# Router logits from the raw stream, an fp32 gather in two halves and a tenth expert slot in a two-block kernel

## The chip, the cores and the metric

The kernel runs on one core of one Trainium2 chip. The metric is the device time of one execution in microseconds, lower is better. A core has a tensor engine (PE), a vector engine (DVE), a scalar engine (ACT), GpSimd (POOL) and a sync engine (SP), which here issues nearly all transfers from memory. Each engine runs its own list of instructions in order; semaphores tie the lists together. Sixteen DMA engines carry the transfers.

## What is computed

256 tokens of width 1024 go through two blocks. The first puts 16 meta tokens ahead, normalizes, mixes (a gated delta rule and a stick-breaking attention), normalizes again and sends every token to 2 of 32 experts; the second is an attention, a squared-relu MLP, a pooling mixer and another MLP. The change lies between the first block's mixer and the end of its experts:

```python
h = layer_norm(DEEPNORM_ALPHA * h + mix, ln1_g[i], ln1_b[i])
ffn = hierarchical_moe(h, ...)
h = layer_norm(DEEPNORM_ALPHA * h + ffn, ln2_g[i], ln2_b[i])
# hierarchical_moe: 4 groups of 8 experts, t = h as tokens
group_probs = softmax(t @ router_group_w + router_group_b); g_idx = argmax(group_probs)
exp_logits = einsum("td,gde->tge", t, router_expert_w) + router_expert_b
top_logit, top_idx = top_k(exp_logits of group g_idx, 2)
top_w = softmax(top_logit) * max(group_probs)
for each expert e: hid = silu(t @ w_gate[e]) * (t @ w_up[e]); y += (hid * weight of e) @ w_down[e]
```

An expert has three fp32 matrices of 1 MB; all 32 are read.

## The kernel before

**Expert stage.** Every expert has 32 places (`CAP`) for its tokens; four experts make a quad, eight quads (`QUADS`) make the stage, two quads a pair. The order is quad 0, quad 1, a spill expert (one expert may have up to 128 more tokens), then quads 2 to 7 (`ORDER`). Of a quad PE computes the up products (L1088, 128x32 tiles, four experts side by side), a turn of the hidden values (L1107, L1111), the down products (L1125) and, after the next quad's up products, the scatter of the result into banks 0 to 3 (L1148), where it is added to the residual stream that `carry` (L1029) has put there through products with the identity. The tokens of a pair come into the expert order by a gather (`gather`, L1057): a product of the normalized stream with a 0/1 matrix `sel` made by `select` (L2170). The stream is held as a rounded part `hiX` (L1606, ACT, in X1) and a remainder `loX` (L2122, DVE, in xT), and the gather multiplies both, each in single-pass fp32r, 256 columns wide. DVE (L2188) and ACT (L1626) copy the four banks to `xs` with scale and shift of the layer norm. `gather_spill` (L1067) does the same for the spill expert right behind quad 0's up products.

**Weights.** They come in units of 2 MB, each two loads of 1024 KB (the second spill unit is half as large): a quad has four up units and two down units, so 48 and 2 of spill. `moe_load` (L530) issues them on SP in the order of use. Seven slots (`MOE_SLOTS`) go round, four in `ring` and three in the arena, and two more places (`once`, in params and in X1 with X2) are used once, so nine units are fetched ahead, in the order `FIRST_USE`, as the mixer's last matrices free their places. After that unit j waits until semaphore `moe_unit` says that the unit seven earlier is used up. `moe_unit` rises by one with each expert's last up product and by two with a quad's down products.

**From the mixer to the experts.** PE ends the `mixed` products (L1010). DVE adds them to the stream and takes statistics (L2100 to L2103), normalizes (L1834); PE fills with four products (`keep_going`, L621), transposes the normalized stream (L628), ACT (L1612) and DVE (L2115) copy it to `xs` with ln1's gain and shift, PE multiplies by the router matrix `wr` (L1023), DVE picks groups, two experts and the membership (L2128 to L2155), makes the remainder of the second tile (L2122), PE counts ranks (L1037 to L1041), DVE makes `select(0)`, PE gathers pair 0. `turned_act`, `turned_dve`, `res` and `four_psum` are counters that later stages use too.

## Time and profile before

| | us |
|---|---|
| median of 3 runs | 1057.35 |
| lowest and highest | 1052.74, 1062.34 |
| the profiled execution | 1054.88 |
| its span in the profile | 1052.8 |
| PE busy in the span | 963.3 (91%) |
| DVE busy | 527.8 (50%) |
| ACT busy | 381.0 (36%) |
| mean granted TensorE clock | 0.965 of full |

The profile is of one execution. The span is the time from its first to its last instruction. Chain of waits means the chain of work that ended last, followed back from the last instruction; a load's piece there is the time from its issue to its landing. PE's fp32 products leave two records each, fp32r products and transposes one. The rows that matter are in the section before the prediction.

### The profile page before, as it was taken

Reading aid. Unit: us, or ns where it says so; the run is one execution under the profiler, and the core shown is the slowest. Engines: PE = TensorE matmul, PEld = TensorE weight load, DVE = VectorE, ACT = ScalarE, POOL = GpSimd, SP = SyncE. Lnnn points to the kernel's source line nnn. Section 1 sums busy time; section 2 is a strip of 40 time slices with the busy share of each in tenths; the row PEclk is TensorE's granted clock in tenths of the full one; section 3 lists DMA queues with packets and bytes.
Section 4 is the critical chain, followed back from the end, with each engine's and each line's share of the span. In section 5 each row is a group of like instructions: output and inputs, shape, how many; then the busy total and the mean of one; then the engine's idle time right before and its main releaser. Section 6 shows DMA issues by size and latency. Waiting matters only on the chain.

```text
span 1052.8 us, 14462 instructions
## 1 busy us (share of the span) xinstructions
PE 963.3 (91%) x6163; PEld 738.7 (70%) x6163; DVE 527.8 (50%) x799; ACT 381.0 (36%) x478; POOL 35.7 (3%) x51
## 2 busy tenths in 40 slices
PE   8999989999999985656979999999999989999997
PEld 7998776455775422213327888899899879999995
DVE  5883463186655102001029568465554665546554
ACT  4554302954322100001036556333433444334341
POOL 1400100012000000000000000000000000000000
PEclk9999999999989988878999999999999999999999
DMA  9733420433773999999997650454554544545421
GB/s 334 235 120 121 160 83 1 151 140 128 301 303 143 416 422 420 422 421 421 421 397 277 209 190 1 182 219 161 192 207 160 173 160 147 199 162 224 172 80 40
DMA packets 67273, 229.42 MB, mean 218 GB/s; under 512 B 4096, under 2 KB 5408, under 8 KB 54544
## 3 DMA queue, kind: packets, MB, share of 16 engines
q1 hardware_dynamic: 65360, 223.28, 55.7%
q0 software_dynamic: 1632, 5.26, 1.5%
q8 instruction: 42, 0.69, 0.3%
q14 instruction: 15, 0.12, 0.0%
q10 hardware_dynamic: 224, 0.07, 0.0%
HBM read 227.54 MB, written 1.05 MB: 217 GB/s over the span
## 4 chain that ended last, share of the span: by engine, by line
PE 80%; DMA 11%; DVE 5%; issue 1%; ACT 1%; SPq 1%; ACTq 0%; DVEq 0%
PE bank L1345 17%; PE bank L1356 16%; PE bank L1088 6%; DMA ring<-in_expert_w_up 5%; PE bank L682 5%; PE bank L706 5%; PE bank L1225 4%; DMA arena<-in_expert_w_up 3%; PE bank L695 3%; PE bank L1010 2%; PE bank L971 2%; PE bank L1287 2%; DMA arena<-in_expert_w_down 2%; PE bank L1229 2%; PE bank L1125 2%; PE bank L715 1%
## 5 line engine op out<-in xcount | busy, mean ns | idle before, releaser
L2341 DVE TENSOR_TENSOR w_lo<-ring,w_hi 128x2048 fp32r<-128x2048 f32 x76 | 170.6, 2288 | 88.1 <-ACT w_hi L1670 87.9
L1670 ACT ACTIVATE w_hi<-ring 128x2048 fp32r<-128x2048 f32 x76 | 141.1, 1909 | 92.8 <-PE bank L1356 86.9
L1345 PE MATMUL bank<-xT_hi,w_hi 128*128 128x256 f32 x512 | 143.8, 281 | 2.6 <-DVE xT_lo L2329 2.6
L1345 PE MATMUL bank<-xT_hi,w_lo 128*128 128x256 f32 x512 | 143.6, 280 | 0.0
L1345 PE MATMUL bank<-xT_lo,w_hi 128*128 128x256 f32 x512 | 143.2, 280 | 0.0
L1356 PE MATMUL bank<-w_hi,hidden_lo 128*128 128x512 f32 x256 | 99.9, 390 | 0.0
L1356 PE MATMUL bank<-w_lo,hidden_hi 128*128 128x512 f32 x256 | 99.8, 390 | 0.0
L1356 PE MATMUL bank<-w_hi,hidden_hi 128*128 128x512 f32 x256 | 99.6, 389 | 0.0
L1345 PEld LDWEIGHTS bank<-xT_hi,w_hi 128*128 128x128 f32 x512 | 96.2, 188 | 3.5 <-issue 3.0
L1345 PEld LDWEIGHTS bank<-xT_lo,w_hi 128*128 128x128 f32 x512 | 96.4, 188 | 0.5
L1345 PEld LDWEIGHTS bank<-xT_hi,w_lo 128*128 128x128 f32 x512 | 95.9, 187 | 0.0
L1088 PE MATMUL bank<-ring,arena 128*32 128x512 f32 x256 | 67.6, 683 | 22.4 <-DMA arena<-in_expert_w_up 22.4
L1088 PE MATMUL bank<-arena 128*32 128x512 f32 x224 | 60.5, 708 | 24.3 <-DMA ring<-in_expert_w_up 24.3
L2239 DVE TENSOR_TENSOR X<-X,bank 128x256 f32<-128x256 f32 x9 | 3.8, 420 | 114.5 <-ACT X L1637 114.5
L1766 ACT ACTIVATE arena<-bank 128x512 f32<-128x512 f32 x32 | 19.2, 600 | 113.1 <-PE bank L1345 113.1
L2442 DVE TENSOR_TENSOR arena<-arena 128x512 f32<-128x512 f32 x32 | 22.1, 690 | 66.8 <-ACT arena L1766 66.8
L1356 PEld LDWEIGHTS bank<-w_hi,hidden_lo 128*128 128x128 f32 x256 | 48.0, 188 | 10.1
L1356 PEld LDWEIGHTS bank<-w_lo,hidden_hi 128*128 128x128 f32 x256 | 48.1, 188 | 9.7
L1356 PEld LDWEIGHTS bank<-w_hi,hidden_hi 128*128 128x128 f32 x256 | 48.1, 188 | 9.6
L1088 PEld LDWEIGHTS bank<-arena 128*32 128x32 f32 x224 | 15.2, 128 | 48.4 <-issue 48.4
L706 PE MATMUL bank<-ring,xT 128*128 128x512 f32 x112 | 48.3, 593 | 0.8 <-issue 0.8
L1637 ACT ACTIVATE X<-bank 128x256 f32<-128x256 f32 x9 | 3.5, 385 | 125.1 <-PE bank L1088 118.7
(527 smaller groups left out, 1675.3 us busy)
## 6 DMA issues: line engine op xcount, KB each, us to landing
ring<-in_mlp_w_up SPq DMA_DIRECT2D x32, 1024.0 KB, 6.9
ring<-in_mlp_w_down SPq DMA_DIRECT2D x32, 1024.0 KB, 6.3
ring<-in_w_in SPq DMA_DIRECT2D x22, 1024.0 KB, 7.5
ring<-in_expert_w_down SPq DMA_DIRECT2D x22, 1024.0 KB, 19.4
ring<-in_expert_w_gate SPq DMA_DIRECT2D x16, 1024.0 KB, 13.8
ring<-in_expert_w_up SPq DMA_DIRECT2D x16, 1024.0 KB, 15.9
arena<-in_expert_w_gate SPq DMA_DIRECT2D x15, 1024.0 KB, 12.3
arena<-in_expert_w_up SPq DMA_DIRECT2D x15, 1024.0 KB, 14.3
```

Of the source, the lines that this page charges most:

```text
L682: last = mm(B[n % 4][:, 0:L], w_[:, k * 512 + c * P:k * 512 + (c + 1) * P], x_[:, k, :], start=(p_ == 0 and k == 0), stop=(p_ == 2 and k = ...
L695: last = mm(B[n % 4][0:r, :], x_[:, k, a:a + r], w_[:, k * 512:(k + 1) * 512], start=(p_ == 0 and k == 0), stop=(p_ == 2 and k == KD - 1))
L706: last = mm(B[n % 4][0:r, :], xT[:, k, a:a + r], slab(u, k), start=(k == 0), stop=(k == KD - 1))
L971: last = mm(B[n], x_(2 * part + kk, i), w_[:, kk * D + half * 512:kk * D + (half + 1) * 512], start=(part == 0 and p_ == 0 and kk == 0), s ...
L1010: last = mm(B[2 * (u - 13) + i], x_, w_, start=(part == 0 and p_ == 0 and kk == 0), stop=(part == 1 and p_ == 2 and kk == 3))
L1088: last = mm(cube(B[4][CAP * e:CAP * (e + 1), :], 2), xs[:, k, (q % 2) * P + CAP * e:(q % 2) * P + CAP * (e + 1)], w_[e][:, :, k, :], start ...
L1225: mm(bank, x_[:, k, i * P:(i + 1) * P], w_hi[:, k * 512:(k + 1) * 512], start=(k == 0 and x_ is xTH), stop=False)
L1345: last = mm(B[4 + (2 * j + pr) % 4][:, cc * SEQ:(cc + 1) * SEQ], w_[:, k * 512 + c * P:k * 512 + (c + 1) * P], x_[:, k, 0:SEQ], start=(k = ...
L1356: last = mm(B[n], h_[:, j % 2, c, i * P:(i + 1) * P], w_[:, c * D + half * 512:c * D + (half + 1) * 512], start=(first and c == 0 and p_ = ...
L1670: act(whi[:, n % 2, half], slot(u)[:, half], ACT.Copy).then_inc(S("split_hi"), 1)
L2341: tt(wlo[:, u % SLOTS, half], slot(u)[:, half], f32(whi[:, n % 2, half]), ALU.subtract).then_inc(S("split_lo"), 1)
L2442: tt(r_, r_, r_, ALU.mult).then_inc(S("square_steps"), 1)
```

## The change

1. **Logits from the raw stream.** PE transposes the stream before it is normalized, as soon as DVE has added the mixer's output (`res` now counts this too, so later uses of `res` are shifted by two), ACT copies it to `xs` unscaled, and PE multiplies by `wr`, which DVE has multiplied by ln1's gain in an earlier stage. DVE then corrects the product: logit = product times 1/std, plus `logit_0`, which is made of mean, 1/std and the column sums `row_1` and `row_0` of the two scaled router matrices. The sums over partitions are one more PE product beside the decay products of the mixer, with a wait for `g_made` 3.
2. **The normalized transposes** for `carry` follow behind the router products, and ACT alone scales all four banks of them. `carry(0)` is split around the rank products; `carry(1)` moves behind quad 0's up products.
3. **fp32 gather.** `hiX` and `loX` are gone. ACT makes a permuted fp32 copy `xhatP` in X1, and the gather multiplies it with an fp32 `sel` in ordinary fp32. The first pair's gather goes in two halves of 128 columns, the second behind quad 0's up products. `gather_spill` moves behind quad 1's up products.
4. **A tenth slot.** xT's place is now free: X0 and the first 2048 columns of xT make a fourth `spare`, `MOE_SLOTS` is 8, and ten units are fetched ahead. The tenth waits for both permuting copies and for the transposes. Thresholds of SP's waits follow from the eight slots. In the overflow case, which these inputs don't take, the sum is kept in X2 instead of X0.
5. **Filling products.** `keep_going(4)` ahead of the transposes and single ones before and after the ranks are gone; ahead of the last quad stand 22 of 128 columns instead of 6 of 512.

In the diff below unchanged lines are left out, and so are hunks that only follow (counter offsets, slot views with the two halves of a unit as a dimension, `pair_weighed`).

```diff
--- before.py
+++ after.py
@@ -230,13 +230,13 @@
...
-    hiX = parts("h1_hi", "X1", 0, NT * D).rearrange("p (i k c) -> p i k c", i=NT, k=KD)
-    loX = parts("h1_lo", "xT", 0, NT * D).rearrange("p (i k c) -> p i k c", i=NT, k=KD)
+    xhatP = X1[:, 0:NT, :].rearrange("p i (k c) -> p i k c", k=KD)
+    spare_sum = cube(X2[:, :], NT)
+    row_1, row_0, row_sums = arena[:, 18820:18856], arena[:, 18856:18892], arena[:, 18892:18964]
+    wr_b, logit_0 = cube(arena[:, 18964:18964 + KD * 36], KD), cube(arena[:, 19252:19324], NT)
...
-    sel = cube(parts("select", "arena", 0, NT * PAIR), NT)
-    reg(NT * PAIR)
-    sel_spill = cube(parts("select_spill", "arena", taken["arena"], NT * SPILL), NT)
-    reg(NT * SPILL)
+    sel = cube(reg(NT * PAIR), NT)
+    sel_spill = cube(reg(NT * SPILL), NT)
...
@@ -331,13 +332,15 @@
...
-    MOE_SLOTS = 7
+    MOE_SLOTS = 8
...
-    once = (params[:, :, :].rearrange("p a d -> p (a d)"), nc.alloc_sbuf_tensor_at("X1_X2", [P, UNIT], F32, offset=placed["X1"] + 4 * NT * D)[:, :])
-    spare = [arena[:, SPARE + a * UNIT:SPARE + (a + 1) * UNIT] for a in range(3)]
-    FIRST_USE = [8, 5, 6, 7, 2, 3, 0, 1, 4]
+    once = (params[:, :, :].rearrange("p (b a) d -> p b (a d)", b=2), nc.alloc_sbuf_tensor_at("X1_X2", [P, 2, HALF_U], F32, offset=placed["X1"] + 4 * NT * D)[:, :, :])
+    spare = [cube(arena[:, SPARE + a * UNIT:SPARE + (a + 1) * UNIT], 2) for a in range(3)]
+    X0_TO_XT = (placed["xT"] - placed["X0"]) // 4
+    spare.append(nc.alloc_sbuf_tensor_at("X0_xT", [P, 2, X0_TO_XT], F32, offset=placed["X0"])[:, :, 0:HALF_U])
+    FIRST_USE = [2, 6, 7, 8, 3, 4, 0, 1, 5, 9]
...
@@ -348,7 +351,7 @@
...
-        return once[m - MOE_SLOTS] if m >= MOE_SLOTS else spare[m - 3] if 3 <= m < 6 else ring[:, {6: 3}.get(m, m), :]
+        return once[m - MOE_SLOTS] if m >= MOE_SLOTS else spare[m - SLOTS] if m >= SLOTS else cube(ring[:, (m + 3) % SLOTS, :], 2)
...
@@ -521,13 +531,16 @@
...
-            elif j in (5, 6, 7):
+            elif j in (6, 7, 8):
...
+            elif j == 9:
+                sp.wait_ge(S("permuted"), NT)
+                sp.wait_ge(S("four_psum"), 8)
...
-                of = U_TWO - 4 + (8, 2, 3, 4).index(j)
+                of = U_TWO - 4 + (2, 3, 4, 5).index(j)
...
-                sp.dma_start(moe_slot(s_, j)[:, a:a + src.shape[1]], src).then_inc(S(f"moe_in{moe_at(s_, j)}"), 16)
+                sp.dma_start(moe_slot(s_, j)[:, a // HALF_U, a % HALF_U:a % HALF_U + src.shape[1]], src).then_inc(S(f"moe_in{moe_at(s_, j)}"), 16)
...
@@ -547,7 +560,7 @@
...
-                sp.wait_ge(S("moe_unit"), FIRST - 6 + (u - U_TWO))
+                sp.wait_ge(S("moe_unit"), FIRST - 7 + (u - U_TWO))
...
@@ -746,8 +759,10 @@
...
-        mm(B[5][:, 24:25], C("mones"), G[:, 8:9], start=True, stop=True).then_inc(S("dec_psum"), 1)
-        pe.wait_ge(S("rows_made"), 1)
+        mm(B[5][:, 24:25], C("mones"), G[:, 8:9], start=True, stop=True)
+        pe.wait_ge(S("g_made"), 3)
+        mm(B[5][:, 32:104], C("ones"), row_sums, start=True, stop=True).then_inc(S("dec_psum"), 1)
+        pe.wait_ge(S("g_made"), 2)
...
@@ -1013,25 +1028,29 @@
...
-        keep_going(4)
-        turn(X0, "xhat", 0, "four_psum")
-        pe.wait_ge(S("router_in"), 16 * (NG + 5))
-        for k in range(KD):
-            if k % 2 == 0:
-                turned(1, k // 2)
-            for i in range(NT):
+        for i in range(NT):
+            pe.wait_ge(S("res"), i + 1)
+            for k in range(KD):
+                last = tr(B[4 + 2 * i + k // 4][:, (k % 4) * P:(k % 4 + 1) * P], X0[:, i, k * P:(k + 1) * P], ident)
+                if k % 4 == 3:
+                    last.then_inc(S("xT_psum"), 1)
+        for i in range(NT):
+            for k in range(KD):
+                if k % 4 == 0:
+                    pe.wait_ge(S("xT_act"), 5 + 2 * i + k // 4 + 1)
...
-        def carry(i):
-            for k in range(KD):
-                mm(B[2 * i + k // 4][:, (k % 4) * P:(k % 4 + 1) * P], xs[:, k, i * P:(i + 1) * P], ident, start=(k % 4 == 0), stop=False)
-        carry(1)
+        turn(X0, "xhat", 0, "four_psum")
+        def carry(i, blocks):
+            for b in blocks:
+                pe.wait_ge(S("turned_act"), 4 + b + 1)
+                for k in (2 * b, 2 * b + 1):
+                    mm(B[2 * i + k // 4][:, (k % 4) * P:(k % 4 + 1) * P], xs[:, k, i * P:(i + 1) * P], ident, start=(k % 4 == 0), stop=False)
...
-        carry(0)
-        keep_going(1)
+        carry(0, (0, 1))
...
@@ -1039,32 +1058,33 @@
...
+        carry(0, (2, 3))
...
-            pe.wait_ge(S(name), total(s_, 9, 8, n // 2 + 1))
-        def gather(s_, p):
-            pe.wait_ge(S("sel_made"), pair_made(s_, p))
+            pe.wait_ge(S(name), total(s_, GATHERS // 2, 2 * NG, n // 2 + 1))
+        def gather(s_, p, first=0, width=PAIR, shift=0):
+            pe.wait_ge(S("sel_made"), pair_made(s_, p) - (1 if width < PAIR and first == 0 else 0))
...
-                    gathered(s_, gather_index(s_, p, 0))
+                    gathered(s_, shift + gather_index(s_, p, 0))
...
+                    at = kk * PAIR + first
...
-                        for m, x_ in enumerate((hiX, loX)):
-                            last = mm(B[(5, 6, 7, 5)[b]][:, kk * PAIR:(kk + 1) * PAIR], x_[:, i, 2 * b + kk, :], sel[:, i, :], start=(i == 0 and m == 0), stop=(i == NT - 1 and m == 1))
+                        last = mm(B[(5, 6, 7, 5)[b]][:, at:at + width], xhatP[:, i, 2 * b + kk, :], sel[:, i, first:first + width], start=(i == 0), stop=(i == NT - 1))
...
-            pe.wait_ge(S("sel_made"), 2)
+            pe.wait_ge(S("sel_made"), 3)
...
+                gathered(None, SECOND + 1 + n)
...
-                        for m, x_ in enumerate((hiX, loX)):
-                            last = mm(B[6 + n][:, c * P:(c + 1) * P], x_[:, i, 4 * n + c, :], sel_spill[:, i, :], start=(i == 0 and m == 0), stop=(i == NT - 1 and m == 1))
+                        last = mm(B[6 + n][:, c * P:(c + 1) * P], xhatP[:, i, 4 * n + c, :], sel_spill[:, i, :], start=(i == 0), stop=(i == NT - 1))
...
@@ -1168,15 +1195,20 @@
...
+                    carry(1, range(4))
+                    gather(None, 0, P, P, SECOND)
+                if q == 1 and s_ is None:
...
+                    gathered(None, SPILL_AT)
+                    gathered(None, SPILL_AT + 1)
...
-                    gathered(None, 4)
-                    gathered(None, 5)
+                    gathered(None, SECOND + 1)
+                    gathered(None, SECOND + 2)
...
@@ -1598,38 +1629,38 @@
...
-        deviation(6, slice(1, 3))
-        def rounded(i):
+        for i in range(NT):
+            for b in range(2):
+                sc.wait_ge(S("xT_psum"), KD + 2 * i + b + 1)
+                act(xs[:, 4 * b:4 * b + 4, i * P:(i + 1) * P], cube(B[4 + 2 * i + b], 4), ACT.Copy).then_inc(S("xT_act"), 1)
+            if i == 0:
+                deviation(6, slice(1, 3))
+        for i in range(NT):
...
-            act(hiX[:, i], X0[:, i, :].rearrange("q (p k) -> q k p", k=KD), ACT.Copy).then_inc(S("h1_round"), 1)
-        rounded(0)
-        for b in (0, 2):
+            act(xhatP[:, i], X0[:, i, :].rearrange("q (p k) -> q k p", k=KD), ACT.Copy).then_inc(S("permuted"), 1)
+        for b in range(4):
...
-        rounded(1)
...
-        def gathered(s_, n, dst, bk, k0):
-            sc.wait_ge(S("xs_psum"), total(s_, 18, 16, n + 1))
+        def gathered(s_, n, dst, bk, k0, apart, first=0):
+            sc.wait_ge(S("xs_psum"), total(s_, GATHERS, 4 * NG, n + 1))
...
-                k, w = k0 + j, dst.shape[2]
-                last = act(dst[:, j, :], bk[:, j * w:(j + 1) * w], ACT.Identity, scale=slot_g[:, k:k + 1], bias=slot_b[:, k:k + 1])
+                k, at, w = k0 + j, j * apart + first, dst.shape[2]
+                last = act(dst[:, j, :], bk[:, at:at + w], ACT.Identity, scale=slot_g[:, k:k + 1], bias=slot_b[:, k:k + 1])
...
-        def gather(s_, p):
+        def gather(s_, p, first=0, width=PAIR, shift=0):
...
-                gathered(s_, gather_index(s_, p, b), xs[:, 2 * b:2 * b + 2, :], B[(5, 6, 7, 5)[b]], 2 * b)
+                gathered(s_, shift + gather_index(s_, p, b), xs[:, 2 * b:2 * b + 2, first:first + width], B[(5, 6, 7, 5)[b]], 2 * b, PAIR, first)
...
@@ -1907,7 +1943,13 @@
...
-        last.then_inc(S("rows_made"), 1)
+        last.then_inc(S("g_made"), 1)
+        per_row = lambda name: by_feature[name].unsqueeze(2).broadcast_to([P, KD, 36])
+        dve.wait_ge(S("router_in"), 16 * (NG + 5))
+        line(tt(wr_b, wr, per_row("ln1_b"), ALU.mult))
+        line(nc.vector.reduce_sum(row_sums[:, 36:72], wr_b.rearrange("p k n -> p n k"), AX.X))
+        line(tt(wr, wr, per_row("ln1_g"), ALU.mult))
+        nc.vector.reduce_sum(row_sums[:, 0:36], wr.rearrange("p k n -> p n k"), AX.X).then_inc(S("g_made"), 1)
...
@@ -1917,6 +1959,8 @@
...
+        nc.vector.tensor_copy(row_1, B[5][:, 32:68])
+        line(tt(row_0, B[5][:, 68:104], rbias, ALU.add))
...
@@ -2097,7 +2141,11 @@
...
-            line(stt(x, x, ALPHA, B[n], ALU.mult, ALU.add))
+            if half:
+                stt(x, x, ALPHA, B[n], ALU.mult, ALU.add).then_inc(S("res"), 1)
+                dve.wait_ge(S("res"), i + 1)
+            else:
+                line(stt(x, x, ALPHA, B[n], ALU.mult, ALU.add))
...
@@ -2108,24 +2156,15 @@
...
+            dve.wait_ge(S("xT_psum"), KD + 2 * i + 2)
...
-        for b in (1, 3):
-            dve.wait_ge(S("four_psum"), 4 + b + 1)
-            for k in (2 * b, 2 * b + 1):
-                last = ts(xs[:, k, :], B[4 + b][:, (k % 2) * SEQ:(k % 2 + 1) * SEQ], by_feature["ln1_g"][:, k:k + 1], by_feature["ln1_b"][:, k:k + 1], ALU.mult, ALU.add)
-            last.then_inc(S("turned_dve"), 1)
-        def low_part(i):
-            dve.wait_ge(S("xhat"), i + 1)
-            dve.wait_ge(S("h1_round"), i + 1)
-            tt(loX[:, i], X0[:, i, :].rearrange("q (p k) -> q k p", k=KD), f32(hiX[:, i]), ALU.subtract).then_inc(S("h1_low"), 1)
-        low_part(0)
-        dve.wait_ge(S("router_in"), 16 * (NG + 5))
+        line(stt(mean_rst, mv[:, 1:1 + NT, 0], -1.0, rst[:, 1:1 + NT], ALU.mult, ALU.mult))
+        for i in range(NT):
+            last = stt(logit_0[:, i, :], row_1, mean_rst[:, i:i + 1], row_0, ALU.mult, ALU.add)
+        line(last)
...
-            last = tt(lg[:, i, :], B[i][:, 0:36], rbias, ALU.add)
+            last = stt(lg[:, i, :], B[i][:, 0:36], rst[:, 1 + i:2 + i], logit_0[:, i, :], ALU.mult, ALU.add)
...
@@ -2154,20 +2193,18 @@
...
-        low_part(1)
...
-        line(nc.vector.tensor_copy(counts, B[4][:, 64:96]))
-        def select(p):
+        def select(p, first=0, n=8):
...
-                slots = C("iota")[:, 0:CAP].unsqueeze(1).broadcast_to([P, 8, CAP])
-                last = tt(cube(sel[:, i, :], 8), slots, rank[:, i, 8 * p:8 * p + 8].unsqueeze(2).broadcast_to([P, 8, CAP]), ALU.is_equal)
+                slots = C("iota")[:, 0:CAP].unsqueeze(1).broadcast_to([P, n, CAP])
+                at = slice(8 * p + first, 8 * p + first + n)
+                last = tt(cube(sel[:, i, CAP * first:CAP * (first + n)], n), slots, rank[:, i, at].unsqueeze(2).broadcast_to([P, n, CAP]), ALU.is_equal)
...
@@ -2175,25 +2212,28 @@
...
-                last = tt(cube(selw[:, i, :], 8), cube(f32(sel[:, i, :]), 8), w_, ALU.mult)
+                last = tt(cube(selw[:, i, :], 8), cube(sel[:, i, :], 8), w_, ALU.mult)
...
-        select(0)
-        def gathered(s_, n, dst, bk, k0):
-            dve.wait_ge(S("xs_psum"), total(s_, 18, 16, n + 1))
+        select(0, 0, 4)
+        select(0, 4, 4)
+        nc.vector.tensor_copy(counts, B[4][:, 64:96]).then_inc(S("router_dve"), 1)
+        dve.wait_ge(S("router_dve"), 5)
+        def gathered(s_, n, dst, bk, k0, apart, first=0):
+            dve.wait_ge(S("xs_psum"), total(s_, GATHERS, 4 * NG, n + 1))
...
-                k, w = k0 + j, dst.shape[2]
-                last = ts(dst[:, j, :], bk[:, j * w:(j + 1) * w], slot_g[:, k:k + 1], slot_b[:, k:k + 1], ALU.mult, ALU.add)
+                k, at, w = k0 + j, j * apart + first, dst.shape[2]
+                last = ts(dst[:, j, :], bk[:, at:at + w], slot_g[:, k:k + 1], slot_b[:, k:k + 1], ALU.mult, ALU.add)
...
-        def gather(s_, p):
+        def gather(s_, p, first=0, width=PAIR, shift=0):
...
-                gathered(s_, gather_index(s_, p, b), xs[:, 2 * b:2 * b + 2, :], B[(5, 6, 7, 5)[b]], 2 * b)
-        gather(None, 0)
+                gathered(s_, shift + gather_index(s_, p, b), xs[:, 2 * b:2 * b + 2, first:first + width], B[(5, 6, 7, 5)[b]], 2 * b, PAIR, first)
+        gather(None, 0, 0, P)
...
@@ -2238,7 +2278,9 @@
...
-                gathered(None, 5, xs_spill[:, 4:8, :], B[7], 4)
+                gather(None, 0, P, P, SECOND)
+            if q == 1 and s_ is None:
+                gathered(None, SPILL_AT + 1, xs_spill[:, 4:8, :], B[7], 4, P)
...
```

## Rows read from the trace of the kernel before

**Rows 1.** The page: busy tenths of the DMA engines, 40 slices of 26.3 us
```profile
DMA  9733420433773999999997650454554544545421
```
**Rows 2.** Windows: stretch, length, busy us by engine, clock, DMA share, GB/s
```profile
316.60:334.00 17.40, 16.93 (x138) 10.46 (x136) 12.43 (x49) 3.91 (x7) 0.00 (x0) 1.00 0.07 15
334.00:538.50 204.50, 148.46 (x925) 60.98 (x924) 23.33 (x62) 22.48 (x45) 0.00 (x0) 0.87 1.01 419
...
332.60:338.00 5.40, 4.36 (x40) 4.09 (x44) 2.49 (x9) 2.49 (x6) 0.00 (x0) 1.00 0.82 284
```
**Rows 3.** Timeline of SP: start, us, issuing line, what it loads, loads merged (x)
```profile
302.81 0.99 SPq L530 DMA_DIRECT2D ring<-in_expert_w_down  x2
332.66 0.33 SPq L530 DMA_DIRECT2D ring<-in_expert_w_gate  x1
...
333.50 8.78 SPq L530 DMA_DIRECT2D ring<-in_expert_w_down  x4
```
**Rows 4.** Chain of waits, 300 to 400 us: start, us, engine and line
```profile
307.58 4.89 PE bank L1023 x32
...
321.52 4.04 PE bank L1057 x32
325.56 7.00 PE bank L1088 x64
332.56 3.73 PE bank L1067 x32
...
337.79 3.64 PE bank L1125 x32
...
348.29 3.96 PE bank L1057 x32
352.26 3.43 PE bank L1148 x8
...
379.12 10.09 PE bank L1088 x64
```
**Rows 5.** The same chain, 400 to 550 us
```profile
517.57 20.95 DMA arena<-in_expert_w_down
...
538.65 5.33 PE bank L1125 x32
```
**Rows 6.** Timeline of DVE and ACT, 298 to 321 us, with idle time before and releaser
```profile
300.48 0.69 DVE L2100 SCALAR_TENSOR_TENSOR X<-X,bank 128x512 f32<-128x512 f32 x1 [1.05 <-PE bank L1010]
...
304.41 2.12 ACT L1606 ACTIVATE h_hi<-X 128x1024 fp32r<-128x1024 f32 x1 [1.94 <-DVE X L1834]
...
306.43 1.92 ACT L1612 ACTIVATE arena<-bank,small 128x256 f32<-128x256 f32 x4
...
312.57 0.30 DVE L2128 TENSOR_TENSOR arena<-bank,arena 128x36 f32<-128x36 f32 x2 [2.73 <-PE bank L1023]
...
317.36 2.00 DVE L2122 TENSOR_TENSOR h_lo<-X,h_hi 128x1024 fp32r<-128x1024 f32 x1
...
320.71 0.76 DVE L2170 TENSOR_TENSOR select<-cst,arena 128x256 fp32r<-128x256 f32 x2
```
**Rows 7.** Chain of waits, 0 to 140 us: fp32 products of 272 and of 128 columns
```profile
17.67 14.67 PE bank L715 x64
...
126.77 1.79 PE bank L785 x16
```
**Rows 8.** Table by windows, around the fall of the granted clock
```profile
306.60:309.90 3.30, 2.32 (x21) 2.35 (x22) 3.24 (x4) 3.30 (x5) 0.00 (x0) 1.00 1.02 429
...
309.90:316.60 6.70, 6.70 (x33) 6.70 (x33) 3.33 (x20) 1.90 (x3) 0.00 (x0) 0.50 1.01 426
```
**Rows 9.** DVE's timeline and the chain of waits near 80 us
```profile
76.87 4.50 DVE L1869 TENSOR_TENSOR w_lo<-ring,first_hi 128x2048 fp32r<-128x2048 f32 x2 [1.01 <-ACT first_hi L1452]
...
86.62 11.12 PE bank L695 x48
```

More of the change, by code:

```diff
@@ L1078, in up_quad @@
         def up_quad(s_, q):
+            if q == 0 and s_ is None:
+                pe.wait_ge(S("router_dve"), 5)
             j = moe_unit(s_, q)
@@ L1119, in down_quad @@
                 moe_landed(s_, j + i)
-            w_ = [moe_slot(s_, j + e // 2)[:, (e % 2) * HALF_U:(e % 2 + 1) * HALF_U] for e in range(4)]
+            w_ = [moe_slot(s_, j + e // 2)[:, e % 2, :] for e in range(4)]
             for half in range(2):
@@ L1649, in experts @@
         def experts(s_, order):
-            gather(s_, 0)
+            if s_ is None:
+                gather(None, 0, 0, P)
+            else:
+                gather(s_, 0)
             for q in order:
```

71 lines of the change are left out of this document (41 added, 30 removed).

## The prediction

> **What bounds the kernel now.** I read the page first. TensorE is 91% busy over the span, but in the middle of the DMA row, from about 330 us to 550 us, every slice but one says 9 [rows 1]. That is the expert stage. The table by windows says it more sharply: from 334.0 to 538.5 us the DMA share is 1.01 at 419 GB/s, while PE is busy for 148 of 204.5 us and at a mean granted clock of 0.87; just ahead of it, from 316.6 to 334.0, the DMA share is 0.07 [rows 2]. So the stage is a full transfer queue that starts late. The reader should see both: a resource with no slack at all for 200 us, and 16 us before it in which the same resource does nothing.
>
> The queue on SP tells why it is empty. The last of nine prefetched units (a unit is 2 MB, two loads of 1024 KB) is issued at 302.81; the next issue is at 332.66 [rows 3], when the first quad's up products end (325.56 + 7.00) [rows 4]: all slots are full until then. In the chain of waits the stage ends with a load issued at 517.57 that lands 20.95 us later, and the down products that it releases at 538.65 [rows 5]. After that the chain is PE work that the change doesn't touch. From the issue at 332.66 to the landing at 538.52 are 205.9 us for what was left. That is 8 quads of 6 units and 2 spill units, one of them half, less 9, is 40.5 units, so **5.08 us a unit**, waits and start included. The end of the stage therefore moves by (change of the restart) + 5.08 us for every unit fetched before it.
>
> **The change, part by part.**
>
> *The tenth slot.* Unit 9 goes behind unit 5, into X0 and the head of xT, which the low part used to hold. SP waits for `permuted` (two permuting copies of 2.12 us on ACT, which begin at 304.41 when the first normalized tile is there [rows 6], so until about 308.7) and for the last transposes. The three units issued from 300.5 to 303.8 keep the queue at work to about 316.6, so unit 9 follows without a hole and lands about 321.7, far ahead of the restart: 39.5 units are left instead of 40.5, **−5.1 us**. It costs nothing on SP, since nothing else is queued behind it but loads that wait for the restart.
>
> *The way to the restart.* Before: the last `mixed` product, statistics, xhat, transposes, scaling copies, router products from 307.58 (4.89 us), logits at 312.57 on DVE, membership, a low part of 2.00 us from 317.36, ranks, select at 320.71 for 0.76 us, gather 321.52 for 4.04 us, up products [rows 4, 6]. After, on the same time axis:
> 1. Raw transposes follow the products: the second tile's residual is made 300.48 to 301.17 [rows 6], so 16 transposes at 0.11 us end by 302.2. ACT's four copies (at most two of L1612's pieces, 0.96 us, each) stay ahead of PE or close to it.
> 2. Router products, 32 passes. At the full clock 21 of them fit in the 2.3 us up to 309.9 (0.11 us each), the other 11 took 2.6 us at half clock [rows 4, 8]. From 302.2: 305.7 at full clock, 307.8 if the clock falls at 303.2. The new correction (three DVE operations of about 0.2 us behind xhat, done at 305.8) is hidden there. Logits at 305.95: 6.6 us earlier.
> 3. DVE from logits to membership, 317.36 − 312.57 = 4.8 us, unchanged: 310.8. The low part of 2.00 us that stood behind it [rows 6] is gone.
> 4. PE is in order, and `carry` for two blocks now stands ahead of the ranks: it waits for ACT, which must finish both permuting copies (308.6) and then four scaling copies at 0.48 us [rows 6]. So 310.5 plus 4 passes: the ranks start at 311.4, not 310.8. This is what is late next. Ten short passes at half clock 2.0 us, rank and a half-sized select 0.9 us, DVE done at 314.3; `carry` of the other two blocks, 8 passes, to 315.1.
> 5. Gather of the first half: 16 products of 128x128 in fp32 are 32 passes. The trace shows 16 such passes in 1.79 us (0.112) and passes of 272 columns at 14.67/64 = 0.229 us [rows 7]. So 3.6 us at full clock, 6.8 at half. The old one took 4.04, 32 single passes.
>
> The clock decides steps 2 to 5. Before, PE was half idle and doing 36-column work from 306.6 to 309.9, and the granted clock stood at 0.50, the 1.2 GHz level, from 309.9 for 6.7 us [rows 8]. The new head has this pattern earlier and longer, and four filling products are taken out. Half clock to 316.6: gather 315.1 to 319.4, up products to **326.6**, −6.0. Clock falling already at 303.2: 327.3, −5.3. Half until 320: about 328.6, −4. Full throughout: 324.6, −8. I take **−5.7 us** and keep −2 to −8.
>
> The clock is where the Trainium skill speaks against the change: its page TensorE: Matmul & The Clock Gate, section Part 4: PE-mode transpose, says that transpose-mode work doesn't count as busy for the clock gate, and here 32 transposes stand where four filling products did. By that rule half clock is likelier through the gather and the first up products; the trace can't separate it, since idle time stands beside the transposes there. It is the first rival's ground.
>
> *Behind the restart.* Queued on PE behind the first up products are now `carry(1)` (16 passes, 1.8 us) and the second gather half (3.6 us) in place of the spill gather (3.73 us) [rows 4]; hidden turn and down products follow, done 10.3 us after the restart against 8.87 before (337.79 + 3.64 − 332.56). The restart issues units 10 and 11: data for 10 us at 419 GB/s, beginning about 1.7 us later (in the 5.4 us from 332.6 on the queue moved 284 GB/s, which is 3.7 us at 419 [rows 2]); unit 12 waits for the down products, so its data begins at +12.2 against an end at +11.7: a hole of 0.5 us. Before, units 9 and 10 covered to 344.4, and of the four loads issued from 333.50 the last was out by 342.28 [rows 3], behind the down products' end at 341.43: a margin of some 2 us. The next two points: up products of quad 1 end at +17.1, queue to +19.7; down products of quad 1 at +37.6 (spill gather 3.6, its copies 1.5, gather of pair 1 in 32 passes of 0.215 = 6.9 instead of 3.96, scatter 3.43, turn 1.3, down 3.7), queue to +39.7 with 1.7 us of start: margin 0.4 us. I add **+0.5 us**, 0 to 4. Later pairs' +2.9 us each lie under DMA: PE has 56 us idle in the stage [rows 2], and eight slots give 5 us more lead than seven.
>
> *Small.* Before the stage, four DVE operations over 288 elements (at most 0.69 us each by the 512-element one of rows 6, so under 2.8) precede low parts that ran from 76.87 to 81.4 behind 1.01 us of idle time, and that PE needs at 86.62 [rows 9]; hidden, with over 3 us to spare. One more PE product and two DVE ones at 113 us: **+0.2 us**. Filling products at the end, 22 of 128 columns (4.9 us) for 6 of 512 (5.1 us): nothing; the last down products took 5.33 us where 3.64 is full clock [rows 4, 5], so ±1.7 by the clock.
>
> **Sum:** −5.1 −5.7 +0.5 +0.2 = **−10.1 us**. The profiled execution took 1054.88 us (span 1052.8), so 1044.8 of its own kind; it lies 2.5 us under the median of the runs, 1057.35, so the forecast is **1047 us**.
>
> **Rivals.**
> - *Only the slot pays.* The clock stays at half through the gather and the first up products, as it did later in the stage: 10.09 us for the same 64 products against 7.00 [rows 4]. Gather end 321.9, up 332.2: −0.4. Total −5.1 −0.4 +0.7: about 1052.5. For it: fewer filling products, transposes. Against: carry and gather are dense from 313.4, and the clock came back at 316.6 after the same kind of stretch. 0.18.
> - *The queue runs dry behind the restart.* The margins of 0.5, 0.9 and 0.4 us fail: any half-clock up product in quad 0 or 1 costs 3 us at one of them, the wait for the spill copies another 1 to 2. Price +4 to +6: about 1052. For it: units 10 to 13 are all that is in flight while PE has 20 us of work between two releases. 0.17.
> - *All of the head is gained*: full clock, −8, no hole: about 1044. 0.10.
> - *Slower: PE becomes the bound of the expert stage.* Odd quads now need up 7.0, gather 6.9, scatter 3.4, turns 1.5, down 3.7: 22.5 us of PE against 6 units, 30 us of DMA. It decides once an odd quad exceeds 30 us, which takes half clock in all of it (43 us, +13 each for three quads, less the prefetched lead of some 15 us): about +14 net of the gains, 1071. Against: the stage ran at 0.87. 0.05.
> - *The forecast*, −7.5 to −12.5 (1045 to 1050): 0.50.
>
> **How the numbers follow.** About 1% (10.6 us) is what a measurement of this kernel can tell from no change, since three runs lay 9.6 us apart. The forecast lies at that bound, so a little under half of its 0.50 counts as faster, with all of the third case and a little of the spread between runs: faster 0.42, same 0.52, slower 0.06. The range takes the forecast, the third case and the first two rivals, with 3 to 4 us for the runs: 1040 to 1056.
>
> **What would show it.** Next issue on SP near 326.5 (the forecast), 332 (first rival). Ten units issued before it, the tenth near 309. Logits near 306. DMA share 1.0 from restart to the last landing near 528; a dip near 338 or 345 to 366 is the second rival. Granted clock 0.5 between 306 and 317. Wrong if the landing moves by less than 5.1 us though unit 9 is early, or if the chain beyond the last down products changes by more than 2 us.

## The result, and the profile after

| | before | after |
|---|---|---|
| median (lowest to highest of 7 runs each), us | 1057.14 (1052.74 to 1062.34) | 1049.38 (1046.36 to 1053.11) |
| ratio after/before, 95% interval | | 0.9943 (0.9918 to 0.9969) |
| profiled execution, us (its span) | 1054.88 (1052.8) | 1053.11 (1050.9) |

The changed kernel is 0.57% faster by this ratio, which is 6.0 us; the medians themselves lie 7.8 us apart. By the bound of 1% that the prediction set this is no change, and the time lies 2.4 us above the forecast. The profiled execution of after is the slowest of its seven, so its span, only 1.9 us under that of before, understates the gain. Two more executions of it were profiled in later comparisons and gave 0.9915 (0.9894 to 0.9936) and 0.9934 (0.9909 to 0.9959). A ratio of about 0.993 over the three is a gain of some 7 us where 10 were forecast.

The chain of waits of after, from the last mixed product to the end of quad 2's up products (start, us, engine and line; L1034 transposes, L1050 `carry`, L1056 to L1059 ranks, L1077 gather, L1112 up products, L1149 down, L1087 spill gather, L1124 and L1159 the spill expert's up and down, L1172 scatter):

```profile
298.95 3.93 PE bank L1025 x17
...
306.00 0.82 DVE X L1870
...
306.84 4.07 ACT X L1640 x2
310.91 1.83 ACT arena L1644 x4
...
312.78 1.23 PE bank L1050 x4
314.00 0.27 PE bank L1056 x2
...
315.98 1.87 PE bank L1050 x8
317.85 4.34 PE bank L1077 x32
322.18 7.00 PE bank L1112 x64
329.19 1.98 PE bank L1050 x16
331.17 3.59 PE bank L1077 x32
...
336.02 3.64 PE bank L1149 x32
339.66 6.87 PE bank L1112 x64
346.53 3.77 PE bank L1087 x32
350.30 1.51 issue
351.81 7.14 PE bank L1077 x32
358.95 3.43 PE bank L1172 x8
...
367.31 7.06 PE bank L1124 x16
374.37 3.43 PE bank L1172 x8
...
378.93 3.70 PE bank L1159 x8
382.63 7.13 PE bank L1112 x64
```

What answers to [rows 4] is the part up to 322.18: the low part and the transposes between the normalized tile and the gather are gone from the chain, and two ACT copies of 4.07 us stand there, with `carry` behind them. From 329.19 on there is one thing that [rows 4] does not have: PE work up to the end of quad 2's up products that no load interrupts. Its gaps and the copies it waits for are 4.3 us in all, the longest 1.51 us at 350.30, where [rows 4] has a wait for a load from 361.03 to 378.87.

SP's timeline of after (start, us, line, what it loads):

```profile
302.90 0.33 SPq L543 DMA_DIRECT2D params<-in_expert_w_gate  x1
...
310.93 0.33 SPq L543 DMA_DIRECT2D X_xT<-in_expert_w_gate  x1
311.30 0.43 SPq L543 DMA_DIRECT2D X_xT<-in_expert_w_up  x1
329.28 1.99 SPq L543 DMA_DIRECT2D ring<-in_expert_w_down  x4
339.88 0.36 SPq L543 DMA_DIRECT2D ring<-in_expert_w_gate  x1
...
389.64 0.33 SPq L543 DMA_DIRECT2D arena<-in_expert_w_gate  x1
```

The load of `params` at 302.90 marks the end of the mixer; before it is at 300.47. Against [rows 3], unit 9 is the new pair at 310.93, and the restart is 26.38 us behind the mark where it was 32.19 (332.66 - 300.47). The mark is the ruler for all that follows, because it splits a span in three: A up to the mark, B from it to the last down products, which the change is about, and C the rest. Restart and B, all in us:

| trace | A | restart, from the mark | B | restart to last down products | C |
|---|---|---|---|---|---|
| before | 300.5 | 32.2 | 238.2 | 206.0 | 514.2 |
| before, again | 298.0 | 33.8 | 240.8 | 207.0 | 514.0 |
| after | 302.9 | 26.4 | 231.2 | 204.8 | 516.8 |
| after, again | 301.4 | 24.0 | 227.5 | 203.6 | 513.8 |
| after, a third time | 303.0 | 26.2 | 231.1 | 204.8 | 514.0 |

In the means B is shorter by 9.6 us (239.5 to 229.9): 7.5 at the restart and 2.1 behind it. The mean span fell by only 5.5, since A was 3.2 and C 0.8 longer. The section after the experiments comes back to both.

The transfers of after by windows (stretch, length, busy us of PE, PEld, DVE, ACT and POOL, clock, DMA share, GB/s):

```profile
341.00:342.00 1.00, 1.00 (x12) 0.32 (x8) 0.08 (x1) 0.00 (x0) 0.00 (x0) 1.00 0.68 156
347.00:348.00 1.00, 1.00 (x11) 1.00 (x10) 0.42 (x1) 0.03 (x1) 0.00 (x0) 1.00 1.02 262
388.00:390.00 2.00, 2.00 (x17) 0.56 (x10) 0.00 (x0) 0.22 (x1) 0.00 (x0) 1.00 0.76 320
390.00:392.00 2.00, 2.00 (x6) 0.94 (x5) 0.42 (x1) 0.16 (x1) 0.00 (x0) 1.00 0.74 180
...
394.00:532.00 138.00, 102.72 (x644) 44.59 (x644) 14.91 (x43) 11.86 (x25) 0.00 (x0) 0.88 1.01 421
```

From 394 on the stage looks like the one of [rows 2]: a full queue at 421 GB/s. Ahead of that the queue is short of work in two places, at 341 and around 390, and the second lasts longer. (At 347 the share is full and only the rate is low. The spill expert's down loads, in halves of 512 KB, come in there, but their size is not the reason: in the run with the changed order, below, the same two loads moved 393 to 410 GB/s at a share of 1.00 to 1.01, from 371 to 373 us. What slows them at 347 stays open.)

### The profile page after: what moved, and what is told of

Its sections match the earlier page's. It is cut to its first block, busy times and chain, and to the rows that moved or that the text cites. A ratio compares the mean times of both kernels' runs of the same rounds, so it can differ in the third digit from the quotient of the medians.

```text
span 1050.9 us, 14628 instructions
## 1 busy us (share of the span) xinstructions
PE 978.8 (93%) x6233; PEld 756.5 (72%) x6233; DVE 526.3 (50%) x808; ACT 386.0 (37%) x490; POOL 33.6 (3%) x51
## 4 chain that ended last, share of the span: by engine, by line
PE 81%; DMA 9%; DVE 5%; ACT 2%; issue 1%; SPq 1%; DVEq 0%; ACTq 0%
PE bank L1376 17%; PE bank L1387 16%; PE bank L1112 6%; PE bank L695 5%; PE bank L719 5%; DMA ring<-in_expert_w_up 4%; PE bank L1256 4%; DMA arena<-in_expert_w_up 3%; PE bank L708 3%; PE bank L986 2%; PE bank L1025 2%; PE bank L1318 2%; DMA X_xT<-in_expert_w_up 2%; PE bank L1260 2%; PE bank L1077 1%
## 5 line engine op out<-in xcount | busy, mean ns | idle before, releaser
L1112 PE MATMUL bank<-arena 128*32 128x512 f32 x224 | 50.2, 672 | 17.6 <-DMA ring<-in_expert_w_up 11.6
L1112 PE MATMUL bank<-ring,arena 128*32 128x512 f32 x192 | 44.0, 723 | 12.9 <-DMA arena<-in_expert_w_up 7.0
L1112 PEld LDWEIGHTS bank<-arena 128*32 128x32 f32 x224 | 12.9, 122 | 39.4 <-issue 39.4
```

The source lines that it names most:

```text
L1112: last = mm(cube(B[4][CAP * e:CAP * (e + 1), :], 2), xs[:, k, (q % 2) * P + CAP * e:(q % 2) * P + CAP * (e + 1)], w_[e][:, :, k, :], start ...
```

## Experiments

The first comparison asks how far two traces of one kernel agree, and what the tenth slot is worth.

**The changed kernel once more.** No edit.

> The changed kernel once more. Theory: its gain lies between the last mixer product and the last down products, where I expect a restart of the loads 26.4 us after that product's end (the end is where the first unit of the last three is issued) and down products of the last quad at about 231 us after it, as in the first trace (329.28 and 534.12 against 302.90). The 2.4 us by which the stage began later in the first trace of the changed kernel, and the 2.9 us lost near 845 us, came from stretches at a granted clock of 0.5 which are not caused by the change: then they should be absent, or elsewhere, in this trace. Rival: they belong to the change (later semaphore counts, one more product in the mixer), and show again at the same places.

Measured 1044.70 us, ratio 0.9915 (0.9894 to 0.9936). Restart 24.0 us behind the mark, B 227.5. The restart comes 2.4 us sooner than in the first trace of the same code. Windows of this trace:

```profile
306.00:310.00 4.00, 4.00 (x23) 3.95 (x22) 2.93 (x18) 4.00 (x4) 0.00 (x0) 0.57 1.01 428
310.00:318.00 8.00, 7.37 (x59) 6.67 (x58) 4.03 (x21) 6.01 (x14) 0.00 (x0) 1.00 1.01 426
```

and of the first one:

```profile
306.80:310.80 4.00, 3.22 (x29) 2.98 (x28) 3.25 (x17) 3.96 (x3) 0.00 (x0) 1.00 1.01 428
...
313.00:319.00 6.00, 6.00 (x29) 6.00 (x30) 1.80 (x11) 3.13 (x7) 0.00 (x0) 0.50 1.00 422
```

Here the granted clock fell early, in the last router products and the transposes of xhat, and was back at 1.00 for `carry`, ranks and gather. There it stood at 0.50, the 1.2 GHz level, through `carry` and ranks and into the gather. The same code gives both.

**Unit 9 fetched late.** The tenth slot exists, but SP waits with it until the restart:

```diff
             elif j == 9:
+                sp.wait_ge(S("moe_unit"), 3)
                 sp.wait_ge(S("permuted"), NT)
```

> The tenth unit is not fetched ahead: its load waits for the first quad's up products like the next ones; eight slots and all else stay. Theory (the slot's 5.1 us are partly eaten by the hole in the loads at quad 2's up products, where PE is late, and by the end, where the last down products wait for PE and ACT and not for their load): the last expert load lands only 3 us later than with the early fetch, since the hole of 2 to 2.5 us closes, and the last down products start 1 to 2 us later, about 232.5 us after the mixer's end. Rival (the slot is worth its full 5.1 us and what is missing was lost in the head): down products 5 us later, 236.

Measured 1047.21 us, ratio 0.9932 (0.9908 to 0.9956), 2.5 us over the unedited kernel on the same chip. From the restart to the last landing 205.7 us with 40.5 units, where the unedited kernel has 203.4 with 39.5. **One unit less makes 2.3 us, not 5.1.** The windows of this trace say where the other 2.7 are. The stretch in which the unedited kernel had a share of 0.75, that is 59 to 63 us behind the restart:

```profile
384.70:386.70 2.00, 2.00 (x17) 0.56 (x10) 0.00 (x0) 0.26 (x1) 0.00 (x0) 1.00 1.00 418
386.70:388.70 2.00, 2.00 (x6) 0.95 (x5) 0.42 (x1) 0.12 (x1) 0.00 (x0) 1.00 1.01 418
```

With a unit more still to transfer the queue has no hole there, and none 12 us behind the restart. Adding up, over 4 us windows, the time by which each stretch falls short of 421 GB/s gives 2.1 us for this kernel (1.7 of it the start) and also for before (2.2), but 4.4 for after (1.6 the start; 0.5 and 0.7 near 341 and 347; 1.6 at 389). What the slot gains as bytes it returns as holes.

**The spill expert behind quad 2.** If the second hole is there because PE reaches quad 2's up products, which free four slots, too late, then they should come sooner:

```diff
-    ORDER = [0, 1, SPILLED] + list(range(2, QUADS))
+    ORDER = [0, 1, 2, SPILLED] + list(range(3, QUADS))
```

(with the unit numbers of `moe_unit` to match).

> The spill expert goes behind quad 2 instead of behind quad 1, so that PE reaches quad 2's up products about 15 us earlier and frees their slots before the queue is empty. Theory: no fall of the DMA share near 388 to 392 us, the last expert load lands 2 to 2.5 us earlier, counted from the restart (203.3 us before, 39.5 units; 201 or less now), and the last down products start 1.5 to 2.5 us earlier if PE's way from the last up weights stays the same. Rival (the 2.5 us are slow loads, not an empty queue): from restart to last landing stays at 203.

Measured 1043.33 us, ratio 0.9905 (0.9887 to 0.9923). Chain and windows of this trace:

```profile
358.65 3.64 PE bank L1149 x32
362.29 6.96 PE bank L1112 x64
369.25 0.23 SPq L543
```

```profile
382.00:394.00 12.00, 10.18 (x27) 4.29 (x25) 1.65 (x6) 1.58 (x3) 0.00 (x0) 1.00 1.01 421
```

The release comes 45 us behind the restart instead of 60, the hole is gone, and restart to last landing falls to 201.0. The cause of the second hole is thereby shown. The gain in time over the unedited kernel, 1.4 us, is less than what medians of four runs can settle; that in the trace, 2.4 us, is not, since restart to last landing is 203.4 us in all three traces of the unedited kernel.

**The table load of the square root behind the copy of `hTs`.** In the first trace of after the last down products did not wait for their weights. Its chain:

```profile
503.33 19.34 DMA arena<-in_expert_w_up
522.66 0.14 issue
522.80 8.87 PE bank L1112 x64
...
532.09 1.28 ACT L1460
...
534.12 5.38 PE bank L1149 x32
```

Up products partly at half clock (8.87 us for 7.00, at a mean of 0.81) and a table load of 1.28 us on ACT. The edit moves the latter behind the copy that the down products need.

```diff
-            if q == QUADS - 1:
-                warm_sqrt()
...
             act(hTs, B[4], ACT.Copy).then_inc(S("hT_out"), 1)
+            if q == QUADS - 1:
+                warm_sqrt()
```

> In the last quad ACT loads the square-root table behind the copy of the turned hidden values instead of ahead of it. Theory (the last down products now wait for PE, DVE and ACT, with the table load of 1.28 us and the 0.2 us behind it in the way): they start about 1.0 to 1.4 us after the hidden values are turned less than before, that is 0.9 us behind the turn instead of 1.3 to 2.1, and the end moves 0.5 to 1.3 us if the load has landed by then. Rival (they wait for the load): no change.

Measured 1043.97 us, ratio 0.9897 (0.9879 to 0.9915). In its trace the last down products waited for their load, at 530.22, as in the unedited kernel beside it, whose chain reads

```profile
501.93 26.89 DMA X_xT<-in_expert_w_down
528.83 0.14 issue
528.96 3.67 PE bank L1149 x32
```

so the edit had nothing to shorten: **inconclusive**. The bound at the tail changes from one execution to the next with the clock of the last up products.

**Filling products in the head.** Eight of 128 columns behind the transposes of xhat, two between the `carry` blocks:

```diff
         turn(X0, "xhat", 0, "four_psum")
+        keep_going(8, 3, P)
...
-        carry(0, (0, 1))
+        carry(0, (0,))
+        keep_going(2, 3, P)
+        carry(0, (1,))
```

> Ten filling products of 128 columns, into a bank that is free there, stand in PE's idle time between the normalized transposes and the rank products (8 ahead of carry, 2 between its blocks). Theory (the restart varies between 24.0 and 26.7 us after the mixer's end in four traces of one head, by where the granted clock stands at 0.5): the clock stays at 1.0 from 310 us on and the restart comes at 24.0 us or earlier. Rival (the clock falls from the narrow router products and the transposes ahead of the idle time, and filling behind them changes nothing): restart at 25 to 26.7 as before.

Measured 1043.88 us against 1055.52 of before beside it, ratio 0.9893 (0.9852 to 0.9934). Windows of this trace:

```profile
306.00:310.00 4.00, 3.84 (x35) 3.68 (x34) 3.26 (x20) 4.00 (x7) 0.00 (x0) 1.00 1.01 426
310.00:318.00 8.00, 7.96 (x71) 6.57 (x73) 3.86 (x19) 5.96 (x12) 0.00 (x0) 1.00 1.01 423
```

Restart 23.7 us behind the mark. In the seven traces of heads without these products and with the gather split it was 24.0 to 26.7, mean 25.9; in the four with them it was 23.7, 23.7, 23.7 and 24.9, mean 24.0. In three of these four the granted clock was 1.00 from 306 to 318 (0.65 from 306 to 310 in the fourth); in none of the seven was it. That is 1.9 us for ten small products that nobody reads. It is a result of the traces alone: no unedited kernel was timed beside this one, and the interval of its ratio holds the 0.9915 and the 0.9934 of the unedited kernel.

**All three:** the order, the table load and the filling products together.

> Three edits at once: spill expert behind quad 2, table load behind the copy of the hidden values, ten filling products in the head. Theory: restart at 24.0 us, 201.0 us from there to the last landing, so last down products at 225.1 us after the mixer's end, against 227.5 and 231.2 of the changed kernel and 238.2 of the one before; ratio to the kernel before about 0.9875. Rival (filling doesn't hold the clock): 226.5 to 228.

Measured 1041.91 us, ratio 0.9874 (0.9849 to 0.9900). Restart 23.7 us behind the mark, B 226.6. Of the 4.7 us by which B lies under the first trace of after, 2.7 are the restart, as with the filling products alone, and 2.0 lie behind it, where the order alone gave 2.4; the last down products here start on PE's work and not on a load (clock 0.88 from 515 to 525 us), so the next gain would have to be sought there.

**The gather of the first pair in one piece.** The opposite test of the hole: the restart is delayed by the second half of the gather, and PE has less to do behind it. The whole pair is gathered before `carry(1)`, in 16 products of 256 columns where the split has 32 of 128. `carry(1)` comes too late here: the copies of the gather have filled its columns of `xs`, and it adds gathered tokens to banks 2 and 3 where the second token tile of the stream belongs. So the kernel leaves out half of the residual stream; the loads and all work behind the gather are as many and as large as before.

> The first pair's gather isn't split: all 256 columns ahead of quad 0's up products, none behind them. Theory: 32 passes of 0.215 instead of 0.112 us put the restart 3.3 us later, at 27.5 to 30; behind it PE has 3.6 us less to do before quad 2's up products, so the hole there, 2.4 us, closes: down products 1 to 2 us later than in the changed kernel, 229 to 232. Rival (a later restart counts in full, the hole is a matter of slots): 231 to 235.

Measured 1045.21 us, ratio 0.9910 (0.9880 to 0.9939). Restart 30.1 us behind the mark, and only 200.8 us from there to the last landing: with 39.5 units, 5.0 under the 205.7 of the late unit 9. With PE early the slot is worth its full price. B is 231.0, as in two traces of the split gather. So splitting the gather brings the restart some 4 us forward, and the holes take back 2.6 of them.

**The order, with unit 9 late.**

> Spill expert behind quad 2 and no early fetch of the tenth unit: beside e2 it gives the slot's worth where no hole takes it. Theory: from restart to last landing 205.9 us for 40.5 units, 4.9 us more than in e2 (201.0), where with the old order the slot was worth only 2.3 us (205.7 against 203.4). Rival (the order itself brings the 2.4 us, slot or no slot): 203.5.

Measured 1048.07 us, ratio 0.9925 (0.9898 to 0.9952); 205.2 us from restart to landing, against 201.0 with unit 9 early and the same order. The slot is worth 4.2 us in this order and 2.3 in the kernel's own. By their ratios the two kernels with unit 9 late are the two slowest of the edited ones, which agrees.

**More filling products at the end, and the changed kernel beside it.** As all three, and 34 filling products in place of 22 ahead of the last quad's up products.

> The three edits together with 34 instead of 22 filling products of 128 columns ahead of the last quad's up products (2.6 us more of them, in a wait of 2.9 us for the weights). Theory (with all three edits the last down products started 226.6 us after the mixer's end, not 225.1, because the granted clock fell in the last up products and PE came later than the load): the clock stays at 1.0 through them, the down products start at the landing, 225.1 us after the mixer's end; ratio to the kernel before about 0.986. Rival (the clock falls there anyway): 226.5, and the same time as before this edit.

> The changed kernel for the third time, on the same chip as the best version. Theory: ratio to the kernel before between 0.991 and 0.994, restart between 24 and 26.7 us after the mixer's end by the granted clock, 203.4 us from the restart to the last landing, and 0.5 to 0.8 per cent slower than the best version. Rival (the gain of the first measurement, 0.6 per cent, is the true one and the second, 0.85 per cent, chance): 0.994 or more.

Measured 1047.04 us, ratio 0.9923 (0.9898 to 0.9948), and 1048.80, ratio 0.9934 (0.9909 to 0.9959). **A miss**: 0.986 was expected. In the traces the stage did gain: B is 227.3 against 231.1 of the unedited kernel beside it, and the last down products started at the landing of their load and ran at full clock (3.67 us), as expected. But restart (24.9 us) and landing (202.4 behind it) came later than the 23.7 and 201.0 that the expectation rests on, and part C was 517.2 us where the other's was 514.0. About half of these 3.2 us arise right behind the stage: PE stood idle for 2.50 us, 14 to 17 us behind the start of the last down products, with nothing in the profile that it waited for, and the other trace lost 1.7 there by slower down products. The other half is the pooling mixer, 11.8 us against 10.1, with a granted clock of 0.66 from 840 to 844 us. Both are code that no edit touches. That accounts for the profiled execution and not for the median; the difference of medians, 1.8 us, is half of what B says, and why it is no more stays open.

**Before, and all three, once more on another chip.** No new edit.

> The kernel before, unchanged, for a second trace of it. If the stage from the end of the mixer to the last down products is set by the transfer queue and hardly by chance, this trace repeats the first one: restart 32 us behind the end of the mixer, last down products 238 us behind it, each within 1.5 us. If the changed kernel's spread (restart 23.98 to 26.38, last down products 227.5 to 231.2) is only the clock's play and was there before too, this trace differs from the first by 3 us or more in one of the two. Ratio 1.000 within 0.3%.

> The kernel of the run that was best so far (order of the spill expert, table load, filling products), unchanged, on another chip. If its 0.9874 was the edits' doing: ratio 0.987 to 0.989, restart near 23.7 us and the last down products near 226.6 us behind the end of the mixer. If it was a lucky chip and the 0.9923 of the kernel with the longer filling is what these edits give: 0.991 to 0.993 and the last down products at 227.5 or later.

Measured 1054.93 us for before, ratio to itself 0.9987 (0.9964 to 1.0009), and 1042.67 for all three, ratio **0.9859** (0.9830 to 0.9888). The 0.9874 repeats, with the restart at 23.7 and B 226.2; the longer filling at the end gave nothing on top. This is the fastest kernel of the study, 13 to 15 us under before by its two ratios, about twice the gain of the change. The second trace of before has B = 240.8, 2.6 more than its first, where at most 1.5 was expected. Of this 1.6 lie ahead of the restart: from 306 to 310 us, in the router products, the granted clock was 0.54 where the first trace has 0.99. The other 1.0 is the end of its chain:

```profile
508.66 18.74 DMA arena<-in_expert_w_up
...
527.53 8.87 PE bank L1088 x64
...
536.82 1.28 ACT L1429
...
538.85 3.69 PE bank L1125 x32
```

These are the slowed up products and the table load of the first trace of after. So the late tail is no cost of the change: both kernels have it in some executions.

## Why the prediction was right, and where it was not

**What bounds the stage: right.** The landing moves with the restart and with the units left. Restart to last landing was 205.9, 205.7 and 205.2 us with 40.5 units where the queue had no second hole (before, unit 9 late in either order). In the first trace of after the last load landed 203.4 us behind the restart, at 532.6: 5.9 us sooner than before on the trace's own axis and 8.3 by the mark, so the sign of being wrong that the prediction set for the landing (less than 5.1) did not show.

**Steps 1 to 5, the way to the restart: right in the first trace, in size and place.** The forecast was -5.7 us, and the first trace has -5.8 by the mark. On its axis, less the 2.43 us by which its mixer ended later, the four scaling copies end at 310.3 (forecast 310.5), the gather begins at 315.4 (315.1), and the restart is at 326.85 (326.6). The late thing was, as step 4 said, ACT: `carry` waits for its copies up to 312.74. But the other traces show that this was one draw among several: -5.8 to -8.2 against the first trace of before, and -7.5 between the means. The head's clock was the widest term, and the range of -2 to -8 held all but the outermost. (In step 2 the sum for a clock that falls at 303.2 is off: 9 passes at full clock and 23 of 0.234 us end at 308.6, not 307.8. That case would end 0.8 later, still inside the range.)

The row-based case of the first rival, half clock through gather and up products, came in none of the seven unfilled heads. The clock did stand at 0.50 through ranks and part of the gather in the first trace, and in the runs with filling products it did not. But the change made the head's clock no worse than it was: from mark to restart its mean is 0.87, 0.93 and 0.87 in the three traces of after, and 0.89 and 0.85 in the two of before, with four filling products and half as many transposes. The Trainium skill says on its page TensorE: Matmul & The Clock Gate, Part 4: PE-mode transpose, that transposes don't count as busy for the clock gate in the way that other products do. What the filling products did agrees with this in direction but does not show it, since they stand in PE's idle time as well as behind the transposes.

**The tenth slot, -5.1: right as bytes, and "Behind the restart", +0.5: the step that failed.** Pairwise, with nothing but unit 9 changed, the two together are -2.3 where -4.6 was forecast. The 0.5 was found where it was put, 12 us behind the restart (0.5 to 0.8 us at 341). A low rate at 347 adds 0.3 over what before has in its like place. What the sum lacks is the 1.6 us at quad 2's up products. The prediction compared PE and queue at the first down products and at quad 1's up and down products, and then covered the rest with "eight slots give 5 us more lead than seven". But the gather of pair 1 grew by 3.2 us (7.14 against 3.96 in [rows 4]), `carry(1)` and half a gather had moved behind the restart, and the spill expert stands between quad 1 and quad 2. Its slots are freed in small parts, and four full ones only when quad 2's up products are done. From SP's timeline of after, PE is there 389.64 - 329.28 = 60.4 us behind the restart. By then the queue has units 10 to 21 to transfer, 11.5 units of 4.98 us (2097 KB at 421 GB/s), with 1.7 us of start and 0.5 of the hole at 341: 59.5. New data come another 1.7 us behind their issue, so by this bookkeeping the hole is 2.6 us; 1.6 were measured. One more line of the same kind as the three that the prediction has would have shown it. The second rival had the right mechanism, but it put it at the three points with small margins, and its price of 4 to 6 us is twice what came.

**Small, +0.2: right where it can be seen.** PE's added product takes 0.28 us. The new filling products at the end are not what makes the tail late: before, with the old ones, has the late tail too.

**The sum.** By the means of the traces: restart -7.5 for -5.7, slot and holes -2.1 for -4.6, together -9.6 for -10.3. Two errors of opposite sign nearly cancel, so that the total fits so well is luck. The timed gain is smaller, some 7 us; in the traces the difference lies in A and C. A was 302.9, 301.4 and 303.0 against 300.5 and 298.0. In the first trace the clock was 0.57 from 240 to 248 us, and 0.79 over 240 to 256 in the third; of the other ten traces with the new head only one, with 0.83, showed a fall there, and neither trace of before did. The nine edited kernels, which have the same code up to the mark, average 299.8, which is in the range of before. So it is likely chance, but two traces of before are too few to exclude 1 us that the change costs ahead of the stage. **That stays open.** C changed by 2.6 us in the first trace (516.8 for 514.2), more than the 2 us that the prediction set as a sign of being wrong; in the other two it was 513.8 and 514.0. The cause is the pooling mixer, code that the change does not touch: 13.02 us from 843.04 on where before took 10.14, at a granted clock of 0.74. In the other traces of the two kernels, C of about 514 comes in two ways: last down products of 5.3 to 5.4 us, partly at half clock, and a mixer of 10.1 (before, after a third time), or 3.7 and 11.7 (before again, after again). The first trace of after has the slow one of both; the only trace with the fast one of both, that of the gather in one piece, has 512.3.

**The chances.** The time lay in the range, and in the case "within 1%", given 0.52. The likeliest case was right in its mechanism, and short of a hole.

## What to carry to other kernels

When a prefetch depth or a release point moves, follow the queue against the engine that frees its slots at every release up to the one where the lead is full again, and not only at the first three: the bytes in flight are spent at each, and the one behind the longest run of engine work decides. Where such a stage has a short piece that frees little (here the spill expert), put it behind one that frees much. And split spans at a landmark before comparing two traces: here chance outside the stage was as large as the effect looked for.

## What the hardware showed that was not expected

- Identical code gave restarts 24.0, 26.2 and 26.4 us behind the same mark, by where the granted clock stood at 0.50. Ten filling products of 0.22 us each, in idle time, made it 23.7 in three traces of four.
- The same 64 up products of the last quad took 7.00 us or 8.87 by the clock, and this decides whether the stage ends on a load or on PE.
- Single stretches of the same code elsewhere lose 2 to 3 us in some executions and none in others (pooling mixer 10.1, 11.7 or 13.0 us), enough to hide a change of 0.3%.
- A full DMA share is not a full rate: from 347 to 348 us the engines were busy throughout (share 1.02) and moved 262 GB/s, in the loads of 512 KB of the spill expert. The same loads moved 393 to 410 GB/s at that share where they stood behind quad 2. No run here shows the cause.
